# The attention bias: added on VectorE beside the row maximum, or accumulated by TensorE in the score bank

## The reference

```python
scores = einsum('bcqhd,bckhd->bchqk', qc, kb) * (Dh ** -0.5)
rel_idx = np.clip(q_pos[:, None] - k_pos[None, :], -MAX_REL, MAX_REL) + MAX_REL
bias = rel_bias[:, rel_idx]
scores = where(valid, scores + bias, finfo.min)
p = softmax(scores, axis=-1)
o = einsum('bchqk,bckhd->bcqhd', p, vb)
```

## Time and profile before

| | value |
|---|---|
| median of 3 runs | 1152.0 us |
| the profiled execution | 1152.0 us, its span 1150.2 us |
| PE busy | 1121.2 us, 97% |
| DVE busy | 609.6 us, 53% |
| ACT busy | 515.6 us, 45% |
| POOL busy | 193.8 us, 17% |
| DMA | 331.99 MB, mean 289 GB/s |
| mean granted TensorE clock | 0.994 |

### The profile page before, as it was taken

The page is one execution under the profiler, slowest core; times in us unless marked ns, Lnnn a source line. Parts: engine busy times, 40 slices in busy tenths (PEclk is TensorE's granted clock), DMA queues, the critical chain, the costliest instruction groups (busy, mean ns, idle before and its releaser), DMA issues.

```text
span 1150.2 us, 18024 instructions
## 1 busy us (share of the span) xinstructions
PE 1121.2 (97%) x7313; PEld 858.4 (75%) x7313; DVE 609.6 (53%) x901; ACT 515.6 (45%) x849; POOL 193.8 (17%) x132
## 2 busy tenths in 40 slices
PE   8999899999799999999999999999999999999996
PEld 7988887999688888878888886666666666666663
DVE  6989966779855695596556642222222222222223
ACT  6565563754365564844665443222333222222223
POOL 1339870313552240400000000000000000000000
PEclk9999999999899999999999999999999999999999
DMA  9862734567547747565447569999999999999994
GB/s 319 268 213 74 258 117 148 207 232 277 209 172 251 261 149 233 158 229 182 147 147 300 200 269 419 424 424 421 426 420 421 424 424 422 425 423 422 426 423 180
DMA packets 82698, 331.99 MB, mean 289 GB/s; under 512 B 4556, under 2 KB 6927, under 8 KB 66111
## 3 DMA queue, kind: packets, MB, share of 16 engines
q1 hardware_dynamic: 81236, 328.43, 73.7%
q0 software_dynamic: 1088, 2.34, 1.0%
q10 hardware_dynamic: 298, 0.11, 0.0%
HBM read 329.83 MB, written 1.05 MB: 288 GB/s over the span
## 4 chain that ended last, share of the span: by engine, by line
PE 80%; DVE 9%; DMA 6%; issue 2%; ACT 2%; POOL 1%; SPq 1%; DVEq 0%; ACTq 0%; POOLq 0%
PE bank L1082 17%; PE bank L441 12%; PE bank L443 11%; PE bank L442 11%; PE bank L1101 9%; PE bank L1072 5%; DMA ring<-in_w_exp_down 3%; PE bank L568 2%; DVE ring_r L1814 2%; DVE arena L1894 2%; DMA ring<-in_w_in 2%; PE bank L1129 1%; POOL ring L2646 1%; DMA ring<-in_w_ada 1%; PE bank L1130 1%
## 5 line engine op out<-in xcount | busy, mean ns | idle before, releaser
L1814 DVE TENSOR_TENSOR ring_r<-ring,arena_r 128x2048 fp32r<-128x2048 f32 x93 | 222.7, 2404 | 133.1 <-ACT arena_r L1302 131.5
L1302 ACT ACTIVATE arena_r<-ring 128x2048 fp32r<-128x2048 f32 x93 | 177.3, 1916 | 150.1 <-PE bank L443 68.2
L2646 POOL TENSOR_TENSOR ring<-ring 128x512 f32<-128x512 f32 x84 | 146.8, 1771 | 224.8 <-ACT ring L1393 196.2
L443 PE MATMUL bank<-arena_r,actT_r 128*128 128x512 f32 x384 | 150.6, 392 | 0.0
L441 PE MATMUL bank<-arena_r,tok_r 128*128 128x512 f32 x352 | 140.9, 400 | 1.7 <-DVE con L2287 1.7
L442 PE MATMUL bank<-ring_r,tok_r 128*128 128x512 f32 x352 | 138.2, 393 | 0.0
L2459 DVE TENSOR_TENSOR arena<-bank,arena 64x512 f32<-64x512 f32 x62 | 42.7, 688 | 175.4 <-PE bank L1101 174.7
L441 PE MATMUL bank<-tok_r,arena_r 128*128 128x256 f32 x352 | 99.5, 283 | 1.9 <-DVE actT_r L1831 1.3
L443 PE MATMUL bank<-tok_r,ring_r 128*128 128x256 f32 x352 | 98.3, 279 | 0.0
L442 PE MATMUL bank<-actT_r,arena_r 128*128 128x256 f32 x352 | 98.2, 279 | 0.0
L2445 DVE TENSOR_TENSOR arena<-bank,arena 128x256 f32<-128x256 f32 x32 | 13.6, 425 | 151.7 <-ACT arena L1733 93.8
(11 more groups left out here) (420 smaller groups left out, 1813.3 us busy)
## 6 DMA issues: line engine op xcount, KB each, us to landing
ring<-in_w_in SPq DMA_DIRECT2D x22, 2048.0 KB, 8.9
ring<-in_w_exp_down SPq DMA_DIRECT2D x22, 2048.0 KB, 21.6
ring<-in_w_exp_gate SPq DMA_DIRECT2D x21, 2048.0 KB, 22.2
arena<-in_w_exp_up SPq DMA_DIRECT2D x21, 2048.0 KB, 23.8
ring<-in_w_ff SPq DMA_DIRECT2D x16, 2048.0 KB, 8.5
ring<-in_w_ada SPq DMA_DIRECT2D x12, 2048.0 KB, 10.9
arena<-in_w_exp_gate SPq DMA_DIRECT2D x11, 2048.0 KB, 21.8
arena<-in_w_exp_down SPq DMA_DIRECT2D x10, 2048.0 KB, 21.5
```

The costliest lines, as they stand in the source:

```text
L443: return mm(o, l[1], r[0], start=False, stop=stop)
L1302: A(hi, w, ACT.Copy).then_inc(S["w_high"], 1)
L1814: TT(half(i, ringR)[0], w, hi.bitcast(fp32), ALU.subtract).then_inc(S["w_rest"], 1)
L2646: i = nc.gpsimd.tensor_tensor(w[:, k, :], w[:, k, :], w[:, k + n, :], ALU.add)
```

## The change

The bias is no longer added on VectorE. TensorE adds it in the bank: after the score product it multiplies the 128x128 block of `bias` (as the stationary operand) with `flip`, the identity with its rows reversed, and accumulates. That is three more 128x128 fp32 products per head, 24 in all, and these use all 128 rows. VectorE then takes only the row maximum, negated, from the bank, in two reductions per head, the second of which waits for the first by a semaphore. ScalarE takes its exponentials straight from the bank with the negated maximum as bias, no longer from the sum that VectorE had written to `aP`; it gives the bank back after both exponentials, where before it did so as soon as the maximum was there. The wait for `bias_masked` goes from VectorE to TensorE.

```diff
--- before.py
+++ after.py
@@ -611,13 +611,18 @@
                 for x in range(2):
                     for t in range(T):
                         wait_read(pe, f"aT{x}{t}")
+                pe.wait_ge(S["bias_masked"], 1)
                 for pr in pairs:
                     two = [(h, 64 * (h % 2), begin(f"as{h}")) for h in (2 * pr, 2 * pr + 1)]
                     for h, pb, bk in two:
-                        mm(bk[:, 0:P], qk4[0][pb:pb + 64, pr, 0:P], qk4[1][pb:pb + 64, pr, 0:P], start=True, stop=True)
+                        mm(bk[:, 0:P], qk4[0][pb:pb + 64, pr, 0:P], qk4[1][pb:pb + 64, pr, 0:P], start=True, stop=False)
                     for h, pb, bk in two:
-                        end(mm(bk[:, P:384], qk4[0][pb:pb + 64, pr, P:256], qk4[1][pb:pb + 64, pr, 0:256], start=True,
-                               stop=True), f"as{h}")
+                        mm(bk[:, 0:P], bias[:, h, 0:P], flip, start=False, stop=True)
+                    for h, pb, bk in two:
+                        mm(bk[:, P:384], qk4[0][pb:pb + 64, pr, P:256], qk4[1][pb:pb + 64, pr, 0:256], start=True, stop=False)
+                    for h, pb, bk in two:
+                        mm(bk[:, P:256], bias[:, h, P:256], flip, start=False, stop=False)
+                        end(mm(bk[:, 256:384], bias[:, h, 256:384], flip, start=False, stop=True), f"as{h}")
 
             def prob_turn(hs):
                 for h in hs:
@@ -1428,12 +1433,13 @@
             def att_exps(hs):
                 for h in hs:
                     act.wait_ge(S["a_max"], h + 1)
-                    act.sem_inc(read[where[f"as{h}"][0]], 1)
-                    step(A(aP[:, h, 0:P], aP[:, h, 0:P], ACT.Exp, scale=-1.0, bias=a_mx[:, 2 * h:2 * h + 1],
+                    bk = wait_full(act, f"as{h}")
+                    step(A(aP[:, h, 0:P], bk[:, 0:P], ACT.Exp, bias=a_mx[:, 2 * h:2 * h + 1],
                            accum_out=a_sum[:, 2 * h:2 * h + 1]))
-                    step(A(aP[:, h, P:384], aP[:, h, P:384], ACT.Exp, scale=-1.0, bias=a_mx[:, 2 * h + 1:2 * h + 2],
+                    step(A(aP[:, h, P:384], bk[:, P:384], ACT.Exp, bias=a_mx[:, 2 * h + 1:2 * h + 2],
                            accum_out=a_sum[:, 2 * h + 1:2 * h + 2]))
                     act.sem_inc(S["a_exp"], 1)
+                    act.sem_inc(read[where[f"as{h}"][0]], 1)
 
             def prob_copies(hs):
                 for h in hs:
@@ -1977,19 +1983,12 @@
                 wait_read(dve, f"mod{c}")
                 tt(o, o, col("bada", 4 * c, 4), ALU.add)
 
-            def bias_blocks(h, b, n):
-                a = bias[:, h, b * P:(b + n) * P]
-                blocks = [list(a.ap[0]), [P, n], [-1, P]] if n > 1 else [list(a.ap[0]), [-1, P]]
-                return bass.AP(a.tensor, a.offset + P - 1, blocks)
-
-            def biased_scores(hs):
+            def largest_score(hs):
                 for h in hs:
                     bk = wait_full(dve, f"as{h}")
-                    V.tensor_tensor_reduce(out=aP[:, h, 0:P], in0=bk[:, 0:P], in1=bias_blocks(h, 0, 1), scale=-1.0,
-                                           scalar=-3 * NEG, op0=ALU.add, op1=ALU.min, accum_out=a_mx[:, 2 * h:2 * h + 1])
-                    V.tensor_tensor_reduce(out=v3(aP[:, h, P:384], 2), in0=v3(bk[:, P:384], 2), in1=bias_blocks(h, 1, 2),
-                                           scale=-1.0, scalar=-3 * NEG, op0=ALU.add, op1=ALU.min,
-                                           accum_out=a_mx[:, 2 * h + 1:2 * h + 2]).then_inc(S["a_max"], 1)
+                    step(V.tensor_reduce(a_mx[:, 2 * h:2 * h + 1], bk[:, 0:P], AX.X, ALU.max, negate=True))
+                    V.tensor_reduce(a_mx[:, 2 * h + 1:2 * h + 2], bk[:, P:384], AX.X, ALU.max, negate=True)\
+                        .then_inc(S["a_max"], 1)
 
             def head_scaled(xt):
                 q = v3(v3(qktok, 4)[:, xt, :], AH)
@@ -2017,10 +2016,9 @@
                         done(TS(v3(aqkT[1], 4)[:, :, t * P:(t + 1) * P], v3(bk[:, :], 4), col("kg"), None, ALU.mult),
                              f"aT1{t}")
                 elif l == 3:
-                    dve.wait_ge(S["bias_masked"], 1)
-                    biased_scores(range(4))
+                    largest_score(range(4))
                 elif l == 4:
-                    biased_scores(range(4, 8))
+                    largest_score(range(4, 8))
                     mod_cols(2)
                 masked(l, 1)
                 corrected(l, 0)
```

## The result

The changed kernel takes 1162.37 us (median of 4 runs, 1162.31 to 1166.04) against 1151.86 us before; the ratio is 1.0093, with a 95% interval of 1.0072 to 1.0113. It is slower, by 10.5 us where 7.4 were forecast. That is the upper edge of the range: on the base of 1152.0 us the ratio gives 1162.7, and the range ended at 1162.5.

What follows compares the result with a forecast made beforehand. TensorE, busy 97% of the span, was taken as the bound. Level 3's +4.03 and level 4's +3.34 gave 7.4 us; 1150.2 + 7.4 + 1.8 = 1159.4 us, range 1155.0 to 1162.5.

Steps and rivals of the forecast that it cites:

- the price of a product: On TensorE, one fp32 bias product is two records of 0.112 us, 0.224 us together.
- a change of shape: On TensorE, going between 64*128 and 128*128 costs 0.09 us leaving and 0.10 entering, 0.19 per change.
- the fill: TensorE's score and bias products of two pairs, at levels 3 and 4: 5.54 us each, 1.51 before.
- VectorE per head: VectorE's two maximum reductions take 0.66 us per head, against 0.56 before; matters for level 4's last heads.
- the remaining wait: At level 4 TensorE's wait for masked(4, 1) shrinks from 1.29 to 0.8 us.
- no wait on a bank: ScalarE's later bank release stays hidden: no TensorE wait at Dt31 or as4, with 3 us of cover.
- the distance that the change makes by itself: Levels 3 and 4 together: 4.03 plus 3.34, 7.4 us slower.
- the 0.4 that I called rounding: Small remainder of both fills' 8.06 us beyond 5.4 of products and 2.3 of shape changes, taken as rounding.
- The first: Rival: TensorE's changes of shape cost nothing more; sum 4.7 us, 1156.7 us; chance 12%.
- second: Rival: TensorE's 6.2 us wait for POOL downstream swallows the delay; 1153.2 us; chance 12%.
- third rival: Late bank release makes as4 wait if ScalarE is over 3 us later; 10.4 us, 1162.4; chance 5%.
- Behind 143.95 all of the chain starts from TensorE, so it is passed on whole: After level 4's last Dt, the whole 7.4 us delay reaches the end of the kernel.

Runs made afterwards that it cites:

- e4: Changed kernel with each fill's score products first, then its bias products grouped; 1160.68 us, ratio 1.0079.
- e3: Changed kernel with TensorE's transposes of ada(7) half a weight chunk later and of ada(9) behind the second of four last products; 1157.25 us, ratio 1.0047.
- e2: Kernel before with TensorE's transposes of ada(7) half a weight chunk later and of ada(9) behind the second of four last products; 1150.14 us, ratio 0.9984.
- e5: Changed kernel with only the transposes of ada(9) 5.5 us later on TensorE; 1158.23 us, ratio 1.0049.
- e6: Kernel before with only the transposes of ada(9) later on TensorE; 1151.22 us, ratio 0.9987.
- e9: Changed kernel with bias products grouped behind each fill's scores and the transposes of both ada(7) and ada(9) later; 1154.49 us, ratio 1.0016.
- e1: Kernel before with 31 idle 128x128 products ahead of level 3's scores, nothing of the change; 1158.81 us, ratio 1.0062.
- e7: Changed kernel without its 24 bias products, so attention is computed without its bias; 1155.98 us, ratio 1.0050.
- e8: Changed kernel with 8 idle 128x128 products ahead of level 3's scores; 1161.1 us, ratio 1.0078.

## Why the prediction was wrong

Right, each within its reading: the price of a product (0.224), of a change of shape (0.19, measured 0.195 by e4), the fill (5.54, measured 5.47), VectorE per head (0.66), the remaining wait (0.8, measured 0.79), no wait on a bank, the distance that the change makes by itself (7.4; 7.1 by e3 less e2, 7.0 by e5 less e6). One small reading of mine was off: the 0.4 that I called rounding is a term. Behind a fill of the changed kernel the next product has the same shape as the last bias product, so the exit and the entry there (0.09 and 0.10) are gone at each level: `ada(2)` comes 3.86 us later from the start of level 3, not 4.03, and `Y41` and `Dt40` begin with no entry (1.95 in place of 2.05). The local sum is 7.2 (150.91 less 131.34, against 143.95 less 131.60). The first, second and third rival were rightly set low: the changes of shape cost their price, the POOL wait of 6.2 us moved with TensorE and took nothing, and no bank release was late. That the third had the price that was measured (10.4, 1162.4) is chance: its wait is not there.

The step that failed is in the sum: "Behind 143.95 all of the chain starts from TensorE, so it is passed on whole." It is passed on whole only where all that meets again is shifted by the same time. `ada(9)` was not. Its load took about 1.2 us longer from issue to ScalarE's start (352.48 to 366.46, in the kernel before 347.27 to 360.06), so POOL began 6.41 us later (371.62 and 365.21), while TensorE was 5.22 late; and POOL's last addition fell under one of VectorE's, 1.88 more. 6.41 + 1.88 - 5.22 = 3.07, what the new wait adds. Then came the half clock, 2.8. The sum had no term for TensorE's clock at all, and it moved twice: 1.4 back behind the wait at `mod7`, 2.8 more behind the one at `mod9`.

I looked for waits that the delay could hide in, and found the one with 6.2 us. What I did not look for were meetings with no slack: in the kernel before, POOL's end at 380.33 and `mod9` at 380.38 are in the trace. The list of TensorE's waits does not show them; the same list for the weight loads does, with two waits for POOL where that has one:

```profile
PEld bank L436 <- POOL ring L2646: 6.9, 2, 6.6
```

The range was too narrow on that side for the same reason: I took its upper end from the local terms.

Open: why the load of `ada(9)` took 14.0 us in the changed kernel and 12.8 in the kernel before. From issue to ScalarE's start it is 13.9 to 14.1 in the changed kernel, its repeat, e3, e4, e5 and e9, and 12.7 to 12.95 in the kernel before, e1, e2, e6, e7 and e8. e8 has the changed attention whole and the short load, so it is not the attention stage's form by itself. The load of feed-forward weights that is issued 0.44 us ahead of it takes longer too (9.1 us to landing in place of 7.8), so it is not `ada(9)`'s load alone. That VectorE's operation came just ahead of POOL's follows from the long load: VectorE's is 5.25 us later than in the kernel before, as TensorE is, and POOL's last addition 6.39. The six profiles with the long load are the six in which that addition takes over 3 us.

## What to carry to other kernels

Moving an addition from VectorE to TensorE costs TensorE its products and, between tile shapes, 0.19 us for each change; group the products by shape. Here even the best form (e9) costs about 4 us more than the addition on VectorE (e2), with 1.29 us of TensorE's time free. Before a delay is called "passed on whole", look for places where two chains meet with no slack, and look in the weight loads' waits too: one with 0.3 us there became 3.1 us, and 2.8 us of half clock behind it. And when POOL is on such a chain, look at what VectorE does beside its last instruction.

## What the runs showed of the hardware

- Behind TensorE's waits of 6.2, 4.9 (e2), 2.9 and 2.02 us (e7) stretches at 1.2 GHz were seen (2.8 and 1.6 us lost behind the latter two), behind those of 1.66 (near 501 us), 1.29 and 0.79 us none. One stretch (e7, 684 us) came without such a wait.
- A fp32 product of a full block beside half-height ones costs 0.19 us at each change; this had the same size in both orders tried.
- One POOL addition (128x512) takes 1.30 us alone and 3.2 to 3.35 under VectorE's 128x2048 addition, which itself goes from 2.29 to as much as 3.39 us (changed kernel).
- A wait that hides under the product before it stands only in the row of the weight load (0.29 us at `mod9` in the kernel before).
